# Two transformer blocks on one core: the norms between the blocks and the dilated values by halves of the tokens

## The reference, cut to what matters

```python
# end of the first block
u = DEEPNORM_ALPHA * x + mix
ple = jax.nn.sigmoid(u @ w_pg[i]) * (p[i] @ w_pp[i])
x = layer_norm(u + ple, ln_g[i], ln_b[i])
# start of the second block
h = rmsnorm(x, g_mix) * (1 + scale) + shift      # scale, shift: from silu(c) @ w_ada + b_ada
q, k, v (dilated); q, k, v (neighbourhood); two gates = split(h @ w_in)
```

## Time and profile before

| what | us |
| --- | --- |
| median of three runs | 2087.15 |
| lowest, highest | 2085.82, 2088.87 |
| profiled execution | 2085.1 |
| its span, first to last instruction | 2083.3 |
| TensorE busy (share of span) | 2016.4 (97%) |
| VectorE, GpSimd, ScalarE busy | 1461.9, 1117.4, 866.8 |
| mean granted clock | 0.989 |

### The profile page before, as it was taken

One profiled execution on the slowest core, in us unless ns is written; L12 is line 12 of the kernel. 1 busy time (PEld: TensorE's weight loads), 2 busy tenths in 40 slices (PEclk: granted clock), 3 DMA queues, 4 the chain that ended last, 5 costly groups with the idle time before them and its releaser, 6 DMA issues.

```text
span 2083.3 us, 28508 instructions
## 1 busy us (share of the span) xinstructions
PE 2016.4 (97%) x10940; PEld 1609.9 (77%) x10940; DVE 1461.9 (70%) x1796; ACT 866.8 (42%) x1401; POOL 1117.4 (54%) x780
## 2 busy tenths in 40 slices
PE   8999999999998999999999999998999999999997
PEld 5878876988875878888866668786788888878885
DVE  7999877631868864443345666867877777788988
ACT  6222263341117144433356770326544444544443
POOL 2585833148872566666533583563887787750000
PEclk9999999999998999999999999999999999999999
DMA  7472481052231533333182203323122222257543
GB/s 296 147 168 86 123 211 55 8 205 81 91 116 49 186 132 134 125 146 132 47 243 66 66 6 121 141 81 121 54 68 91 91 83 70 71 198 245 178 143 115
DMA packets 85094, 249.68 MB, mean 120 GB/s; under 512 B 16807, under 2 KB 23767, under 8 KB 83775
## 3 DMA queue, kind: packets, MB, share of 16 engines
q1 hardware_dynamic: 70704, 189.70, 27.7%
q10 hardware_dynamic: 11184, 40.65, 5.3%
q0 software_dynamic: 3072, 17.51, 3.1%
HBM read 191.30 MB, written 54.56 MB: 118 GB/s over the span
## 4 chain that ended last, share of the span: by engine, by line
PE 75%; DVE 16%; ACT 3%; POOL 2%; issue 2%; DMA 1%; SPq 0%; ACTq 0%; DVEq 0%; POOLq 0%
PE ps L3814 31%; PE ps L3934 8%; PE ps L3432 7%; DVE back L2579 6%; PE ps L3750 4%; PE ps L3851 4%; PE ps L3890 3%; PE ps L359 2%; PE ps L552 2%; PE ps L382 1%; PE ps L530 1%; PE ps L3397 1%; PE ps L3585 1%; PE ps L520 1%; DVE h_high L2663 1%
## 5 line engine op out<-in xcount | busy, mean ns | idle before, releaser
L1994 POOL TENSOR_TENSOR up_parts<-front,up_parts 128x512 fp32r<-128x512 f32 x120 | 189.2, 1586 | 73.9 <-ACT up_parts L2314 73.1
L3934 PE MATMUL ps<-ffn_parts,w_parts 128*128 128x512 f32 x924 | 212.6, 392 | 5.1 <-DVE ffn_parts L3218 5.1
L3934 PEld LDWEIGHTS ps<-ffn_parts,w_parts 128*128 128x128 f32 x924 | 174.2, 189 | 42.9 <-DVE w_parts L3210 3.8
L3814 PE MATMUL ps<-t_high,up_parts 128*128 128x512 f32 x640 | 204.0, 389 | 1.3 <-ACT back L2321 0.8
L1994 POOL TENSOR_TENSOR gate_parts<-front,gate_parts 128x512 fp32r<-128x512 f32 x96 | 137.9, 1438 | 105.0 <-ACT gate_parts L2314 105.0
L3814 PE MATMUL ps<-tg_high,gate_parts 128*128 128x512 f32 x512 | 167.7, 395 | 3.5 <-POOL gate_parts L1994 2.6
L2579 DVE TENSOR_TENSOR back<-back 128x256 f32<-128x256 f32 (+10 forms) x105 | 139.6, 1329 | 23.4 <-ACT back L2221 15.1
L3814 PE MATMUL ps<-h_high,up_parts 128*128 128x512 f32 x480 | 154.8, 389 | 0.3 <-DVE back L2990 0.2
L3814 PEld LDWEIGHTS ps<-t_high,up_parts 128*128 128x128 f32 x640 | 120.2, 188 | 27.2 <-issue 1.4
L1930 POOL TENSOR_TENSOR w_parts<-front,sb_zero 128x1024 fp32r<-128x1024 f32 x25 | 56.1, 2244 | 142.6 <-PE ps L3750 56.5
L2321 ACT ACTIVATE back<-ps 128x512 f32<-128x512 f32 x128 | 75.8, 592 | 130.8 <-PE ps L3814 130.8
(11 more groups left out here) (461 smaller groups left out, 5244.1 us busy)
## 6 DMA issues: line engine op xcount, KB each, us to landing
front<-w_up SPq DMA_DIRECT2D x44, 512.0 KB, 4.4
front<-w_ada SPq DMA_DIRECT2D x32, 512.0 KB, 3.6
front<-w_down SPq DMA_DIRECT2D x22, 512.0 KB, 3.7
back<-w_down SPq DMA_DIRECT2D x22, 512.0 KB, 4.5
front<-w_in SPq DMA_DIRECT2D x16, 512.0 KB, 4.0
front<-w_out SPq DMA_DIRECT2D x16, 512.0 KB, 5.3
residual<-back ACTq DMA_DIRECT2D x2, 4096.0 KB, 16.5
back<-w_ada SPq DMA_DIRECT2D x16, 512.0 KB, 5.7
```

Of the source, the lines that this page charges most:

```text
L1994: pool.tensor_tensor(parts[:, BANK:], src, parts[:, 0:BANK].bitcast(F32), ALU.subtract)\
L3814: mm = pe.matmul(o, parts[:, at + k * P:at + (k + 1) * P], x, start=p in (1, 2, 5) and k == 0 and q == 0, stop=k == 3 and q == 2, skip_gro ...
L3934: mm = pe.matmul(ps[:, (4 if p in (2, 5, 3) else 0) + m, :], weights[:, w_ * BANK + m * P:w_ * BANK + (m + 1) * P], half_of(x, x_), start= ...
```

## The change

The work between the last two projection tiles and the dilated values is done for tokens 0 to 511 (half 0) first and then for 512 to 1023 (half 1).

The projection tiles 6 and 7 go as 6 half 0, 7 half 0, 6 half 1, 7 half 1 (`half_tile`); half 0's mean sum and its spread stand inside 6 half 1. The running sum ends at tile 5; tiles 6 and 7 enter the mean sum on their own. The sums are of 128 tokens in place of 256 (`half_sum`), four matmuls each. The spread (`half_spread`) is four matmuls with full 128 x 128 weights `PICKS`, which VectorE makes with five memsets, all to one bank. Every operation of 1024 tokens in this stretch is one of 512 per half, so there are twice as many.

The dilated values are done half by half: 96 matmuls on banks 0 to 3, then 96 on banks 4 to 7. Inside the first 96 stand half 1's statistics: two tiles of them after each k of the first two weight blocks, half 1's layer-norm spread after block 2, its RMS spread after the first k of block 3. The weight blocks are thus used twice, so all four are kept: two more pairs of pages (`WR_V`), and GpSimd makes all four before the values. The neighbourhood values' first two blocks are split when half 1 reaches its third block.

The spill is two DMAs of 2 MB, one after each half. ScalarE's `gate_t_high(3, 2)` comes after the copy of the dilated values.

```diff
+        WR_V = rounded_pages("w_parts_values", (40, 41, 12, 13), 4)
+        def values_parts(b):
+            n = nth(b)
+            if b < B_V2:
+                return WR_V[2 * (b - B_V1 - 2):2 * (b - B_V1 - 1)] if b >= B_V1 + 2 else (WR[n % 2], WR[3 - n % 2])
+            return WR[n % 2], WR[2 + n % 2]
...
+                    elif B_V1 < b < B_V2 + 2:
+                        pool.wait_ge(S("w_used"), B_WOUT + whole(B_V1 + 1) + (1 if b >= B_V2 else -1))
...
-            pool.wait_ge(*T("pg_tile", 9))
+            pool.wait_ge(S("ple_ready"), 9)
+            split(B_V1)
+            pool.wait_ge(*T("pg_tile", 10))
             pool.memset(page(22)[0:HEADS2, :], MASKED).then_inc(S("pool_step"), 1)
             pool.dma_start(page(20, 2)[0:33, :], t["onehot"]).then_inc(S("onehot_landed"), 16)
-            pool.wait_ge(S("ple_ready"), 9)
-            split_stage(B_V1, 4, 1)
+            pool.wait_ge(S("ple_ready"), 10)
+            for b in range(1, 4):
+                split(B_V1 + b)
             split_stage(B_V2, 4, 1)
...
+            half_gate(6, 0)
+            half_gate(7, 0)
+            half_square(0, 0)
+            half_square(0, 1)
+            half_gate(6, 1)
+            half_gate(7, 1)
             ada_read(24, 8)
+            for k in range(2, FT):
+                half_square(0, k)
             act.activation(stat[:, 0:1], eps[:, 0:1], ACT.Sqrt)
-            squares_act(act, "ln_1", FT, lambda k: X2[:, k, :], 0, True, TEMPS_3)
...
+                        if h == 0 and what[0] == "h" and what[1] < 4:
+                            half_square(1, 2 * what[1])
+                            half_square(1, 2 * what[1] + 1)
+                    if h == 0 and what == ("h", 5):
+                        half_std(1)
+                    elif h == 0 and what == ("h", 6):
+                        root_mix(1)
+            mixed(0)
+            act.dma_start(x_spill[:, :, 0:BANK], HV[:, :, 0:BANK]).then_inc(S("half_spilled"), 16)
+            mixed(1)
+            act.dma_start(x_spill[:, :, BANK:], HV[:, :, BANK:]).then_inc(S("spilled"), 16)
...
-            gate_t_high(3, 2)
             act.wait_ge(S("spilled"), 16)
+            act.wait_ge(*T("half_spilled", 16))
             act.wait_ge(S("dist_in_dram"), 16)
             values_out("dil")
+            act.wait_ge(S("dil_v_tiles"), FT)
+            gate_t_high(3, 2)
...
+            half_gated(6, 0)
+            half_gated(7, 0)
+            half_mean(0)
+            half_centred(0, 0)
+            half_centred(0, 1)
+            half_gated(6, 1)
+            for k in range(2, FT):
+                half_centred(0, k)
+            half_gated(7, 1)
             modulation_1()
...
+            half_mean(1)
+            for k in range(4):
+                half_centred(1, k)
...
+                        if h == 0 and what == ("l", 5):
+                            root_1(1)
+                            mean_square(1)
+                        elif h == 0 and what == ("l", 6):
+                            rstd_mix(1)
...
+            def half_tile(m, h, w_high, w_low, high, low, give_back, columns, between, done):
+                for k in range(FT):
+                    if k in columns:
+                        ada_column(columns[k], "raw_used")
+                    for n, (w_, x_) in enumerate(((w_high, high), (w_high, low), (w_low, high))):
+                        mm = pe.matmul(ps[:, 2 * (m % 2) + h, :], w_[:, k * P:(k + 1) * P], half_of(x_[k], h),
+                                       start=k == 0 and n == 0, stop=k == FT - 1 and n == 2)
+                        if give_back and k == 0 and n == 0:
+                            mm.then_inc(S(give_back), 1)
+                    if k < FT - 1 and k in between:
+                        between[k]()
+                mm.then_inc(S(done), 1)
+            def half_sum(bank, at, weights, x, start, stop):
+                for j in range(4):
+                    mm = pe.matmul(ps[32 * j:32 * j + 32, bank, at * P:at * P + P], weights, x[:, P * j:P * j + P],
+                                   start=start, stop=stop)
+                return mm
+            def half_spread(bank, x):
+                for j in range(4):
+                    mm = pe.matmul(ps[:, bank, P * j:P * j + P], PICKS[:, j, :], x, start=True, stop=True)
+                return mm
+            def mean_sum(h):
+                pe.wait_ge(S("tile_added"), FT - 3)
+                pe.wait_ge(S("ple_ready"), FT + 2 * h)
+                for q, x in enumerate((X2_SUM, X2[:, 6, :], X2[:, 7, :])):
+                    mm = half_sum(MEAN_BANK[h], 0, ones[:, 0:32], half_of(x, h), q == 0, q == 2)
+                mm.then_inc(S("norm_mean"), 1)
+            def mean_spread(h):
+                pe.wait_ge(S("norm_stat_read"), 2 + h)
+                half_spread(MEAN_SPREAD[h], HALF_MEAN).then_inc(S("norm_mean_spread"), 1)
+            def half_stats(h, first, n):
+                for k in range(first, first + n):
+                    pe.wait_ge(S("norm_square"), tiles_to("ln_1", FT * h + k + 1))
+                    half_sum(SQUARE_BANK[h], 1, ones[:, 0:32], HALF_TEMPS[k % 4], k == 0, k == FT - 1)
+                    half_sum(G2_BANK[h], 2, SUM_G2[:, k, :], HALF_TEMPS[k % 4], k == 0, k == FT - 1)\
+                        .then_inc(S("norm_square_used"), 1)
...
+                if base == B_WPG:
+                    for m, h, back, columns, between in ((6, 0, "w_used", {0: 28}, {}), (7, 0, None, {2: 29}, {}),
+                                                         (6, 1, None, {6: 30}, {3: lambda: mean_sum(0), 6: lambda: mean_spread(0)}),
+                                                         (7, 1, "w_used", {}, {})):
+                        if h == 0:
+                            pe.wait_ge(S("w_split"), nth(base + 2 * m) + 1)
+                            pe.wait_ge(S(free), m - 1)
+                        half_tile(m, h, *w_parts_1(base + 2 * m), high, low, back, columns, between, done)
...
-            pe.wait_ge(S("tile_added"), FT - 2)
-            sum_tiles(pe, 0, ones[:], X2_SUM, True, False)
-            pe.wait_ge(S("ple_ready"), FT + 1)
-            sum_tiles(pe, 0, ones[:], X2[:, FT - 1, :], False, True).then_inc(S("norm_mean"), 1)
-            pe.wait_ge(S("norm_stat_read"), 2)
+                           {2: {4: 25}, 3: {}, 4: {2: 26, 4: 27}, 5: {}})
+            for k in range(FT):
+                pe.matmul(ps[:, 7, 0:1], ones[:], B_SQUARE[:, k:k + 1], start=k == 0, stop=k == FT - 1)
             pe.wait_ge(S("ada_read"), 3)
-            spread_tiles(pe, TEMPS_3[2][:, 0:256]).then_inc(S("norm_mean_spread"), 1)
-            for k in range(FT):
-                mm = pe.matmul(ps[:, 3, 256:257], ones[:], B_SQUARE[:, k:k + 1], start=k == 0, stop=k == FT - 1)
-            for k in range(FT):
-                pe.wait_ge(S("norm_square"), tiles_to("ln_1", k + 1))
-                sum_tiles(pe, 2, ones[:], TEMPS_3[k % 2], k == 0, k == FT - 1)
-                sum_tiles(pe, 3, SUM_G2[:, k, :], TEMPS_3[k % 2], k == 0, k == FT - 1).then_inc(S("norm_square_used"), 1)
-            for k in range(FT):
-                if k == 5:
-                    pe.wait_ge(S("norm_rstd"), norms_to("ln_1"))
-                    spread_tiles(pe, TEMPS_3[2][:, 256:512]).then_inc(S("norm_spread"), 1)
-                sum_tiles(pe, 1, SUM_GB[:, k, :], X2[:, k, :], k == 0, k == FT - 1).then_inc(S("norm_square_used"), 1)
+            half_stats(0, 0, 2)
+            mean_sum(1)
+            half_stats(0, 2, 2)
+            mean_spread(1)
+            half_stats(0, 4, 4)
+            rstd_spread(0)
             pe.wait_ge(S("relb_landed"), 16)
             pe.wait_ge(S("onehot_landed"), 16)
...
+            def values(A, base, half):
                 for b in range(4):
                     pe.wait_ge(S("w_split"), nth(base + b) + 1)
-                    if A == "dil" and b == 0:
-                        for k in range(2):
-                            pe.wait_ge(S("norm_ready"), y_ready(k, "h"))
-                            for t in range(8):
-                                products_of(b, k, t, ((0, HH), (2, HH)))
-                        for k in range(2):
-                            pe.wait_ge(S("h_split"), k + 1)
-                            for t in range(8):
-                                products_of(b, k, t, ((0, HL),))
-                        continue
+                    high, low = values_parts(base + b)
                     for k in range(2):
                         if A == "dil":
-                            pe.wait_ge(S("h_split"), 2 * b + k + 1)
-                        for t in range(8):
+                            pe.wait_ge(S("h_split" if half else "u_split"), (0 if half else FT) + 2 * b + k + 1)
+                        for t in range(8) if A == "na" else range(4 * half, 4 * half + 4):
                             if A == "na" and b == 0 and k == 0 and t % 2 == 0:
```

(20 more changed lines are left out.)

272 lines of the change are left out of this document (144 added, 128 removed).

## The result

The changed kernel takes 2098.6 us (median of 4, 2095.12 to 2100.45) against 2086.49 us for the kernel before on the same chip: ratio 1.0066, 95% interval 1.0052 to 1.0080. It is 0.66% slower, where the forecast was 2086.4 us in a range of 2082.3 to 2091.0, with 0.14 for slower: the forecast was wrong. The profiled execution took 2100.45 us, span 2098.6.

What follows compares the result with a forecast made beforehand. TensorE was taken to bound the kernel, so its waits before the dilated values count. Halves free 8.9 us and pay back 5.0 + 1.7 + 0.2 + 0.7, plus 0.5 spill wait: -0.8, time 2086.4 us, range 2082.3 to 2091.0.

Steps and rivals of the forecast that it cites:

- 0.14 for slower: Chance of a slower kernel: 0.09 for the second spill landing late, 0.05 for statistics sums inside the values costing more.
- Tiles end 1.5 later: Projection tiles: mean sums 0.6 us and spread 0.85 put between them move their end to 617.4; tile 7's earlier start costs zero.
- Serial part, values at 639.5: Statistics, roots, reciprocals and scalings between tiles and dilated values: values start at 639.5 us, 8.9 earlier than before.
- The 3.0 for GpSimd's splits: Before the values: VectorE loses 3.0 us to GpSimd's weight splits, bounds 0 and 4, tile 7's second half included.
- z1: Serial part: VectorE operation with two SBUF sources, due at 632.4, held by a GpSimd split until 634.3, 1.9 us.
- The clock in the first statistics: Rival, 0.22: TensorE's clock also falls in the first half's statistics after the tiles, +2.5 us, 2088.9, no change.
- the 642 that I gave as its sign: Sign of the clock falling in the first statistics: the first dilated-values matmul comes beyond 642 us.
- First half 31.2, then a stall of 0.7: Dilated values: first half with second-half statistics takes 31.2 us, clock loss 2.5 included; 0.7 stall before the second half.
- Behind it: After the dilated values: VectorE's last l at 683.8, its cover suffices; 0.5 us spill wait, weight blocks in time.
- My own sign of being wrong: Wrong if values start before 636 or TensorE stands over 2 us between half tiles or the two kinds of values.
- The late spill: Rival, 0.09: the second spill takes 16.5 us to land, delaying ScalarE's copy and the neighbourhood values, +7.0 us, 2093.4.

Runs made afterwards that it cites:

- h_mean_late: Changed kernel with the first half's mean sum behind the seventh instead of fourth product pair of tile 6's second half, its spread later too: 1.0062 of the kernel before.
- g_hold_b3: Changed kernel with GpSimd's split of the last dilated weight block (3) held until VectorE's sixth l of the first half: 1.0058 of the kernel before.
- a_copies: Changed kernel with VectorE's four copies of dilated values behind the second gate sum, no longer the third: 1.0035 of the kernel before.
- c_hold_v1: Changed kernel with GpSimd's splits of dilated weight blocks 1 to 3 held until after VectorE's first l of the first half: 1.0069 of the kernel before.
- b_hold_v2: Changed kernel with GpSimd's splits of neighbourhood weight blocks 1 to 3 held until after VectorE's third gate sum: 1.0047 of the kernel before.
- k_all: Changed kernel with a_copies, g_hold_b3 and h_mean_late together, plus six second-half statistics tiles ahead of the values: 2085.17 us against 2083.51, 1.0003 of the kernel before.
- n_best: k_all with second-half spreads one step earlier, some centrings and squares earlier, eight unread matmuls in the last wait before the values: 2082.69 us, 0.9991 of the kernel before.
- e_early: Changed kernel with four of the second half's eight statistics tiles ahead of the dilated values: 1.0053 of the kernel before.
- l_fill: Changed kernel with 15 matmuls whose result nobody reads in TensorE's two waits ahead of the dilated values: 1.0067 of the kernel before.

## Why the prediction was wrong

Step by step, in the order of the sum:

- *Tiles end 1.5 later.* They end 3.9 later. The two things I priced were near (mean sum 0.79 against 0.6, spread 0.81 against 0.85, by the starts around them); TensorE's wait of 1.90 for tile 7's gating I had at zero. VectorE's gating was slowed by GpSimd's modulation sums, which I had not looked at for this place. h_mean_late shows that this wait hides others and is worth nothing alone.
- *Serial part, values at 639.5.* From the tiles' end it took 25.1 in place of 22.1. The 3.0 for GpSimd's splits were about right (g_hold_b3 gives 3.1 back by moving one block), but the operation hit was a tensor_scalar of 128 columns and not the z1 that I named. Two things were missing. The three blocks of splits follow tile 7's second gating, which came late with the tiles, so they run from 30.0 to 43.0 us and not from 27.8 to 40.6, and the tensor_scalar is held until the last of them ends. And what follows the tensor_scalar was too cheap: from its end to the first value matmul the changed kernel, a_copies, c_hold_v1 and g_hold_b3 all take 8.5 us, while my sum has 6.5 from the end of the short operations (630.0) to a start at 636.5. It took that start ahead of its own first l at 637.6, and the trace has the first value matmul wait for that l (3.97 <-DVE h_low): 1.1 us. VectorE's wait of 0.97 for ScalarE's copy of the mixed spread, a spread made at half clock, is most of the rest.
- *The clock in the first statistics.* It was at 0.50 for 626 to 628, so the rival came true, and the values, 51.5 from tile 6's start or 644.9 on the time axis of before, lie beyond the 642 that I gave as its sign. But it was not the cause: a_copies and b_hold_v2 have a clock of 1.0 through these statistics and start their values at the same 51.5, for the end of block 3's split decides.
- *First half 31.2, then a stall of 0.7.* It took 33.2 and 1.05. Sums at 0.22 and the clock's 2.7 were near their prices (0.21 and 2.5). The switch between values and sums was not: one k's twelve products with two statistics tiles take 4.43 us (657.16 to 661.59), 12 x 0.227 + 6 x 0.218 = 4.03 of it work. Four such groups lose 1.6 us.
- *Behind it, the step that failed most:* "VectorE finishes its last l at 683.8 ... 7.6 of this cover goes, none is missing." Counted from the second half's start, the last l ended after 14.3 us, not 12.4: 0.9 of these 1.9 is the split beside it (1.58 in place of 0.69), the rest ScalarE's pace of 2.02 a tile. The gate sums took 12.7, not 9, for GpSimd's splits on them. Together 27.0 against a second half of 21.8: 5.2 missing. TensorE waited 3.59 of it (the first four tiles of the neighbourhood values cover the rest), the clock at half behind that wait took some 1.8 more. My own sign of being wrong, TensorE standing more than 2 us between the two kinds of values, is nearly this wait; it stands four tiles later. I had counted VectorE's cover down to half a microsecond of its end and left the two prices in it at what they are without the new neighbours. That needed a rival of its own, since it ends on the slower side, and there was none. It is not the whole loss: with this tail repaired alone (a_copies, 1.0035) the kernel is still slower than before.
- *The late spill* was the wrong rival for slower: 7.3 us to landing, and ScalarE's copy at 700.04 was ahead of the second half's end at 703.4.

Each miss is 2 to 5 us and all have the same sign: waits, contention and switches that I had taken at zero or at the cheap end, and one slip of 1.1 in my own sum. The mechanism of the gain was right: the stretch before the values shrank from 32.5 to 25.0, and with the repairs to 24.6. What the halves pay back inside the values is larger than its gain unless the neighbours are re-ordered. k_all at 1.0003 and n_best at 0.9991 show that, once the tail, one split and the place of six tiles are put right, the idea is worth next to nothing or a tenth of a per cent.

Open: how often the clock falls at each place. Of the eight profiles with the 1.90 wait, two (c_hold_v1, e_early) have it at half behind the wait (1.55 us), six have not, and l_fill's executions differ by 5 us. The splits' cost at tile 7's gating and the fixed part of ScalarE's 512-wide forms were read in the trace and not tried by themselves.
